# A woven mixer in a two-block transformer kernel: the order of the input blocks, the order within each engine's queue, and where the recurrent steps stand

## What is computed

```python
h = rmsnorm(x, mix_pre_gain)
proj = einsum('bsd,de->bse', h, w_in)                 # 2048 -> 5376
q_a, k_a, v_a, q_r, f_r, i_r, g_r = split(proj)       # 1024,128,128, then 4 x 1024
attn = rmsnorm(sliding_window_attention(q_a, k_a, v_a, sinks), attn_out_gain)   # 16 heads of 64
# recurrent part, 8 heads of 128
f = lb + (1 - lb) * sigmoid(f_r); log_f = log(f); key = 1 - f; qf = silu(q_r); vf = i_r
# per head: outputs o from decayed products of qf and key with vf and a carried state
o = o * rsqrt(mean(o * o) + EPS) * norm_gain
rnn = o * silu(g_r)
mixed = einsum('bse,ed->bsd', concatenate([attn, rnn]), w_out)
x = x + rmsnorm(mixed, mix_post_gain)
```

## Time and profile before

| | |
|---|---|
| time, median of 3 runs (range) | 2494.46 us (2490.78 to 2499.16) |
| the profiled execution's own time, and its span | 2494.21 us, 2492.4 us |
| granted TensorE clock, mean | 0.977 of 2.4 GHz |
| busy: PE, DVE, ACT, POOL | 96%, 59%, 46%, 2% |
| chain that ended last, by engine | PE 85%, issue 7%, DVE 4%, ACT 2%, DMA 1% |

### The profile page before, as it was taken

How to read it: one execution, slowest core, us unless ns; L and a number is a source line. 1 busy time by engine, 2 the same in 40 slices (tenths; PEclk the granted TensorE clock), 3 DMA queues, 4 the chain that set the end, 5 groups by cost and what they waited for, 6 DMA issues and landing times.

```text
span 2492.4 us, 33962 instructions
## 1 busy us (share of the span) xinstructions
PE 2389.5 (96%) x12206; PEld 1997.0 (80%) x12206; DVE 1461.0 (59%) x1849; ACT 1151.8 (46%) x1612; POOL 42.7 (2%) x65
## 2 busy tenths in 40 slices
PE   6999977999999999999999998989999999999997
PEld 5888856888888888888888786778888888888886
DVE  4444367557777546777566566765666544566544
ACT  4444245445555435555454454444544434444442
POOL 1000100000000000000010000000000000000000
PEclk9999878999999999999999899999999999999999
DMA  7666341646556665665655342336566666666652
GB/s 231 192 193 186 92 152 36 194 144 186 177 184 194 194 192 178 187 193 191 202 157 182 93 145 76 102 111 203 153 191 183 192 192 190 187 183 189 208 192 101
DMA packets 311149, 419.19 MB, mean 168 GB/s; under 512 B 15518, under 2 KB 206312, under 8 KB 310292
## 3 DMA queue, kind: packets, MB, share of 16 engines
q1 hardware_dynamic: 308032, 407.09, 53.5%
q0 software_dynamic: 2448, 8.75, 1.1%
q10 hardware_dynamic: 580, 2.20, 0.2%
HBM read 415.86 MB, written 2.12 MB: 168 GB/s over the span
## 4 chain that ended last, share of the span: by engine, by line
PE 85%; issue 7%; DVE 4%; ACT 2%; DMA 1%; POOL 0%; DVEq 0%; SPq 0%; POOLq 0%; ACTq 0%
PE PS L1521 22%; PE PS L1487 12%; PE PS L1486 12%; PE PS L1485 12%; PE PS L1522 11%; PE PS L1717 4%; PE PS L1718 2%; PE PS L1730 1%; PE PS L1732 1%; PE PS L1731 1%; PE PS L1811 1%; DVE x L1076 1%; ACT work L760 1%; PE PS L1539 1%; DMA stage<-in_w_in 1%
## 5 line engine op out<-in xcount | busy, mean ns | idle before, releaser
L1521 PE MATMUL PS<-actT,whi 128*128 128x512 f32 x2432 | 861.3, 398 | 2.8 <-DVE wlo L961 2.8
L932 DVE TENSOR_TENSOR wlo<-stage,whi 128x1024 fp32r<-128x1024 f32 (+1 forms) x367 | 440.1, 1204 | 485.1 <-ACT whi L596 485.1
L1522 PE MATMUL PS<-actT,wlo 128*128 128x256 f32 x2432 | 683.9, 281 | 0.0
L596 ACT ACTIVATE whi<-stage 128x1024 fp32r<-128x1024 f32 (+1 forms) x367 | 381.3, 1042 | 544.0 <-PE PS L1487 519.2
L1521 PEld LDWEIGHTS PS<-actT,whi 128*128 128x128 f32 x2432 | 457.9, 188 | 116.5 <-DVE wlo L961 3.4
L961 DVE TENSOR_TENSOR wlo<-stage,whi 128x1024 fp32r<-128x1024 f32 x298 | 362.7, 1223 | 239.2 <-ACT whi L654 239.0
L654 ACT ACTIVATE whi<-stage 128x1024 fp32r<-128x1024 f32 x298 | 315.9, 1061 | 322.2 <-PE PS L1522 308.4
L1522 PEld LDWEIGHTS PS<-actT,wlo 128*128 128x128 f32 x2432 | 457.3, 188 | 0.1
L1487 PE MATMUL PS<-whi,gT 128*128 128x512 f32 x864 | 340.4, 394 | 0.0
L1486 PE MATMUL PS<-wlo,gT 128*128 128x512 f32 x864 | 338.7, 392 | 0.0
L1485 PE MATMUL PS<-whi,gT 128*128 128x512 f32 x864 | 335.2, 388 | 0.0
(11 more groups left out here) (288 smaller groups left out, 2239.9 us busy)
## 6 DMA issues: line engine op xcount, KB each, us to landing
stage<-in_w_up SPq DMA_DIRECT2D x304, 512.0 KB, 3.8
stage<-in_w_down SPq DMA_DIRECT2D x216, 512.0 KB, 4.1
stage<-in_w_in SPq DMA_DIRECT2D x168, 512.0 KB, 3.7
stage<-in_w_out SPq DMA_DIRECT2D x64, 512.0 KB, 4.4
stage<-in_cmp_k_w SPq DMA_DIRECT2D x8, 512.0 KB, 4.2
stage<-in_cmp_v_w SPq DMA_DIRECT2D x8, 512.0 KB, 5.4
x<-in_x ACTq DMA_DIRECT2D x2, 1024.0 KB, 7.0
grow<-bias_by_distance POOLq DMA_DIRECT2D x2, 1024.0 KB, 7.8
```

Of the source, the lines that this page charges most:

```text
L596: nc.scalar.activation(whi[:, s % SPLITS, 0:wd], stage[:, s % STAGES, 0:wd], ACT.Copy)\
L932: nc.vector.tensor_tensor(wlo[:, s % SPLITS, 0:wd], stage[:, s % STAGES, 0:wd], whi[:, s % SPLITS, 0:wd].bitcast(F32), ALU.subtract).then_ ...
L1521: nc.tensor.matmul(o, whi[:, j % SPLITS, at], actT[:, k, :], start=k == 0, stop=False)
L1522: last = nc.tensor.matmul(o[:, S:2 * S], wlo[:, j % SPLITS, at], actT[:, k, 0:S], start=False, stop=k == KC - 1)
```

## The change

- The order of the blocks: all eight forget and query blocks follow the attention's queries (tiles 24 to 55), then both halves of IR (56 to 71), then the gates (72 to 87). The banks of the last three blocks and the waits for them follow.
- `WINDOW_AT`: a head every 3/2 tiles from 24 (last at 46), before every 5/4 from 25 (last at 43). `STEP_AT`: step r at 63 + 7r/5 (63 to 84), before 57 to 82 with a gap in the middle. Its last `values` and `o_out` come after the loop.
- The two sets of sigmoids stand at 53 and 60 (before 52 and 68), logs at 55 and 62, PE's transposes of them at 55 and 61.
- In ACT's and DVE's loops the mixer operations come ahead of the copies of an ended block.
- `turn_mix2` for p = 0 and 1 moves from the last tile to positions 84 and 86, both into bank 0, and ACT and DVE split these four chunks in iterations 87 and 89. The sigmoid of the first gates moves from 86 to 88, that of the second behind the loop.

```diff
-IN2_BLOCKS = [("tok", C_KA, 256)] + [("feat", C_QA + 256 * i, 256) for i in range(4)] + [("tok", C_IR, NW)]
+IN2_BLOCKS = [("tok", C_KA, 256)] + [("feat", C_QA + 256 * i, 256) for i in range(4)]
 for _i in range(4):
     IN2_BLOCKS += [("feat", C_FR + 256 * _i, 256), ("feat", C_QR + 256 * _i, 256)]
-IN2_BLOCKS += [("tok", C_IR + NW, NW), ("tok", C_GR, NW), ("tok", C_GR + NW, NW)]
+IN2_BLOCKS += [("tok", C_IR, NW), ("tok", C_IR + NW, NW), ("tok", C_GR, NW), ("tok", C_GR + NW, NW)]
...
-IN2_BANKS = [(2 * (k % 2), 2 * (k % 2) + 1) for k in range(14)] + [(0, 3), (2, 0), (3, 2)]
-WINDOW_AT = {25 + 5 * s // 4: s for s in range(HA)}
-STEP_AT = {n: r for r, n in enumerate((57, 59, 60, 62, 63, 65, 66, 68, 72, 73, 75, 76, 78, 79, 81, 82))}
-MIX2_BANK = (4, 5, 6, 7, 2, 3, 4, 5)
+IN2_BANKS = [(2 * (k % 2), 2 * (k % 2) + 1) for k in range(14)] + [(0, 2), (3, 0), (2, 3)]
+WINDOW_AT = {24 + 3 * s // 2: s for s in range(HA)}
+STEP_AT = {63 + 7 * r // 5: r for r in range(16)}
+MIX2_BANK = (0, 0, 6, 7, 2, 3, 4, 5)
...
+                if n - 7 in STEP_AT:
+                    o_out(STEP_AT[n - 7])
+                if n - 3 in STEP_AT:
+                    decays(STEP_AT[n - 3])
+                if n - 5 in WINDOW_AT:
+                    window_turned(WINDOW_AT[n - 5])
+                if n - 4 in WINDOW_AT:
+                    window_exp(WINDOW_AT[n - 4])
+                if n == 52:
+                    attention_squares()
+                if n in (53, 60):
+                    sigmoids(n // 60)
+                if n in (55, 62):
+                    logs(n // 62)
+                if n in (58, 64):
+                    logs_turned(n // 64)
+                if n in (87, 89):
+                    split_turned("mix2", range(n - 87, n - 85), MIX2_BANK)
+                if n == 88:
+                    gate_sigmoid(0)
                 ended = in2_end(n - 3)
                 if ended in FEAT_NO:
                     low_sums2(ended)
                 if ended in TOK_NO:
                     tokens_out(ended)
...
+            o_out(HR * TT - 1)
+            gate_sigmoid(1)
...
-            split_turned("mix2", range(12), MIX2_BANK)
+            split_turned("mix2", range(4, 12), MIX2_BANK)
...
-                if n in (54, 70):
-                    logs_turn(n // 70)
+                if n in (55, 61):
+                    logs_turn(n // 61)
...
-                if n == IN2_TILES - 1:
-                    for p in range(2):
-                        turn_mix2(p)
+                if n in (84, 86):
+                    turn_mix2((n - 84) // 2)
                 in2_tile(n)
+            values(HR * TT - 1)
             for p in range(2, 6):
                 turn_mix2(p)
```

More of the change, by code:

```diff
@@ L802, in tokens_out @@
                 for t in range(TT):
-                    if t == 0 and k >= 14:
-                        act.wait_ge(ev("first_half"), k - 13)
+                    if t == 0 and k >= 13:
+                        act.wait_ge(ev("first_half"), k - 12)
                     else:
@@ L810, in sigmoids @@
             def sigmoids(g):
-                act.wait_ge(ev("in2_feat"), 4 + 4 * (g + 1))
+                act.wait_ge(ev("in2_feat"), 8 + 4 * g)
                 hs = slice(4 * g, 4 * g + 4)
@@ L1404, in _ @@
                     root_of_x(3, 6)
-                ended = in2_end(n - 3)
-                if ended in FEAT_NO:
-                    join2(ended)
                 if n == 12:
@@ L1419, in _ @@
                     front2(WINDOW_AT[n - 3])
-                if n == 51:
+                if n == 53:
                     attention_root()
-                if n == 53:
+                if n == 55:
                     attention_scaled()
[L1424 to L1427, removed]
+                if n in (53, 60):
+                    forgets(n // 60)
+                if n in (56, 63):
+                    keys(n // 63)
                 if n - 5 in STEP_AT:
@@ L1431, in _ @@
                     products(STEP_AT[n - 3])
[L1432 to L1437, removed]
-                    gated(0)
+                if n == 80:
+                    mean_square(0, hstat[:, 0, 0:8], hstat[:, 1, 0:8], P, "o_out", 8)
+                if n in (87, 89):
+                    split_turned("mix2", range(n - 87, n - 85), MIX2_BANK)
+                if n == 88:
+                    gate_silu(0)
+                if n == 89:
+                    gated(0)
+                ended = in2_end(n - 3)
+                if ended in FEAT_NO:
+                    join2(ended)
+            mean_square(0, hstat[:, 0, 8:16], hstat[:, 1, 8:16], P, "o_out", 16)
+            gate_silu(1)
             def last_chunks(j):
@@ L1443, in last_chunks @@
                     split_turned("mix2", range(12, KC), MIX2_BANK)
-            split_turned("mix2", range(8), MIX2_BANK)
+            split_turned("mix2", range(4, 8), MIX2_BANK)
             gated(1)
@@ L1701, in in2_tile @@
                     pe.wait_ge(ev("in2_join"), FEAT_NO[12] + 1)
-                elif j == 0 and k == 16:
-                    pe.wait_ge(ev("in2_tok"), 2 * TOK_NO[14] + 2)
+                elif j == 0 and k > 14:
+                    pe.wait_ge(ev("in2_tok"), 2 * TOK_NO[k - 2] + 2)
                 elif k < 14 and j == 0 and k >= 2:
@@ L1720, in in2_tile @@
                     for t in range(TT):
-                        if t == 1 and j == 0 and k == 14:
-                            pe.wait_ge(ev("in2_join"), FEAT_NO[13] + 1)
-                        if t == 1 and j == 0 and k > 14:
+                        if t == 1 and j == 0 and k >= 14:
                             pe.wait_ge(ev("in2_tok"), 2 * TOK_NO[k - 1] + 1)
@@ L1732, in in2_tile @@
                             last = nc.tensor.matmul(o, al, h, start=False, stop=at_k == KC - 1)
-                        if t == 0 and j == 7 and k >= 14:
+                        if t == 0 and j == 7 and k >= 13:
                             last.then_inc(ev("first_half"), 1)
@@ L1752, in logs_turn @@
                 else:
-                    pe.wait_ge(ev("fac"), 8)
+                    pe.wait_ge(ev("logf_out"), 1)
                 for t in range(TT):
@@ L1790, in exponents @@
                     pe.wait_ge(ev("mix2_in"), 64)
-                if r % 8 == 0:
-                    pe.wait_ge(ev("logf_out"), r // 8 + 1)
-                    pe.wait_ge(ev("key_done"), r // 8 + 1)
+                if r == 0:
+                    pe.wait_ge(ev("logf_out"), 2)
+                    pe.wait_ge(ev("key_done"), 2)
                 if r >= 1:
@@ L1834, in turn_mix2 @@
                 if p == 0:
-                    pe.wait_ge(ev("fac"), HR * TT)
+                    pe.wait_ge(ev("in2_tok"), 8)
+                if p == 1:
+                    pe.wait_ge(ev("actlo_mix2"), 2)
                 if p == 2:
@@ L1839, in turn_mix2 @@
                     pe.wait_ge(ev("in2_tok"), 10)
-                if p >= 6:
-                    pe.wait_ge(ev("actlo_mix2"), 2 * (p - 5))
+                if p == 6:
+                    pe.wait_ge(ev("fac"), HR * TT)
                 pe.wait_ge(ev("mixed2"), 2 if p < 4 else p // 2 + 1)
```

## The result

The changed kernel takes 2459.57 us (median of 4 runs, 2457.81 to 2461.18) against 2494.82 for the kernel before beside it (4 runs); the ratio is 0.9864 with a 95% interval of 0.9844 to 0.9883. The forecast was 2460. The profiled execution has a span of 2459.4 us and took 2461.2.

The account below looks back on a forecast made before the run. PE, busy 96% of the span, was taken as the bound, so gains come from its waits and low clock: 23.1 + 13.0 - 1.5 = 34.6 us off 2494.2 gives 2459.6, say 2460; range 2453 to 2478.

Parts of the forecast that it names:

- Waits, 23.1 less 1.5 for new ones: PE's waits in windows (7.2), steps (12.9) and before the output product (3.0) go; 1.5 us of new short waits come.
- eight lines: The list of PE's waits on other engines in the kernel before, summing to 23.1 us.
- Clock, 13 us (12 to 15): Window and step stretches: PE's low clock follows waits and goes with them, gaining 13 us, bounds 12 to 15.
- The order of the queues: ACT and DVE loops: mixer operations ahead of block copies remove the windows' 7.2 us of waits, bounds 5.7 to 7.2.
- Turns: Before the output product: turning and splitting four chunks earlier removes PE's wait of 3.0 us, bounds 1.5 to 3.0.
- Blocks and sets out of the steps: Step stretch: moving feature blocks and second sigmoid set out removes waits of 8.1, 1.6 and 0.8 us.
- the spacing of the windows: Window stretch: heads every 3/2 tiles instead of 5/4 remove the 1.5 us wait on DVE's wout.
- Cover at position 61: Second logarithm set: ACT needs 8.9 us, PE arrives after 11.0, slack 2.1 us, so nothing waits.
- A: Rival, windows: clock falls whatever the waits, from small matmuls and transposes; gain 25.2 us, time 2469; chance 0.14.
- B: Rival, steps: DVE becomes what PE waits for; 15 us of the gain lost, time 2475; chance 0.12.
- C: Rival: no effect, PE loses the same time to other waits one copy later; 2490 to 2498 us; chance 0.03.
- D: Rival, steps: low clock takes the stretch, costing 59 us over half of positions 63 to 88; 2519 us; chance 0.05.

Follow-up runs that it names:

- e3: Changed kernel with the first four chunks turned ahead of the last tile and split after the loop, as before; stage 340.7 us against 338.4.
- e6: Changed kernel with a recurrent step at every tile from 63 to 78, sixteen in a row; stage 337.6 us against 338.4.
- e10: Same kernel as e7 run again, on one chip with the changed kernel; 2451.43 us against 2456.0, ratio to before 0.9822.
- e12: Same kernel as e2, profiled a second time; 2477.1 us, stage 361.0 us.
- e2: Changed kernel with the old queue order, block copies ahead of mixer operations in both loops; 2475.54 us in one run, stage 357.3 us.
- e1: Kernel before with only the new queue order, mixer operations ahead of block copies; 2468.09 us against 2491.3, ratio 0.9908, stage 348.2 us.
- e4: Changed kernel with the old window spacing, a head every 5/4 tiles from 25; stage 338.36 us.
- e8: Kernel before with one swap in ScalarE's loop, o_out ahead of the next step's decays; 2492.75 us, stage 369.4 us.
- e5: Changed kernel with PE's second transposes of the logarithms at position 59, not 61; stage 343.7 us against 338.4.
- e7: Changed kernel with chunks 12 to 15 turned ahead of the output product's fifth tile, not its seventh; 2449.03 us, ratio to before 0.9834.

## Why the prediction was right

The forecast was a gain of 34.6 us; the medians give 35.3 and the profiled stage 38.2. Term by term:

- **Waits, 23.1 less 1.5 for new ones.** Right: all eight lines are gone. The 0.75 us at tile 3 is not the change's: it stands in nine of the fourteen profiles, the second one of before among them, and is absent from the first of before, e3, e6, e10 and e12. The allowance of 1.5 was not needed.
- **Clock, 13 us (12 to 15).** In the profile that I read the stage had 30.7 us at 0.50, which cost at most 15.4 (the rest, 15.8, less 0.17 for each of twelve waits is 13.8); in a second profile of the same kernel 20.5, at most 10.2. The bounds were for one profile; the term varies by 5 us between runs, more than they allowed. That it goes to zero with the waits was right in every profile without a long wait. That each wait has such a price was wrong as a rule, as e2 shows.
- **The sum came out closer than its terms.** In the profiles, 3.6 us too little in the stage met a late start of the profiled stage of 5.2 us. The start ranged from 1281.2 to 1289.1 us over fourteen profiles with the same code ahead of it, so agreement within 1 us is partly luck, and the forecast of 34.6 should be held to the stage's 38.2 (34.1 between the second profiles).
- **Which part does what.** The order of the queues was the main cause, as argued, and carries more than I had given it: of the waits I had put 7.2 + 2.4 = 9.6 us down to it, and e1 without any other part lost 14.9 (23.1 less the 5.2 among the steps and the 3.0 before the output product). In stage that is 28.4 us added to before, and 18.9 or 22.6 taken out of the changed kernel (e2, e12), so the parts don't simply add. Turns 3.0, as computed (e3). Blocks and sets out of the steps: what is left of 38.2, 9.8 us behind e1, less 3.0 for the turns, so 6.8, made up of e1's 5.2 us of waits among the steps and its rest of 1.6. This one is a difference, not a run of its own, and it doesn't tell the blocks from the sets. I had put 10.5 us of waits down to it (8.1, 1.6 and 0.8).
- **A wrong reason with no effect on the sum.** I put the 1.5 us on `wout` down to the spacing of the windows. The spacing does nothing (e4); in e1 these waits go with the old spacing. The chain of before shows DVE's join of a block (L1275, L1279) directly ahead of `wout`:

```profile
1418.06 0.69 DVE QRT L1279
1418.76 0.40 DVE wout L1333 x2
1419.15 0.14 issue
1419.29 0.52 PE PS L1776 x3
```

- **Cover at position 61.** Computed 2.1 us; in the changed kernel the logarithm ends near 1482.0 and PE's transposes start at 1483.93, 1.9 us. e5 took two tiles (5.5 us) away and showed a wait of 3.5, so 2.0. The Trainium skill's "ScalarE: Activation LUTs", What ACT_TABLE_LOAD costs, gives a drain for each switch of tables, by which e5's wait would have been 6.2 us (an estimate from its 1380 ns); the runs don't show that drain.
- **Rivals.** A (the clock falls in the windows for the small matmuls and transposes themselves): with all of them in place and no waits it stands at 1.00 in the changed kernel, e1, e4 and e6, so what Part 4 of the Trainium skill's "TensorE: Matmul & The Clock Gate" says of transposes explains no fall here. B (DVE): refuted by e6 even at the closest spacing. C (it does nothing) is refuted by the result; its idea, that a removed wait uncovers another, held in e8 and in part in e1. D needed a fall of the clock in the steps without a wait; none occurred.

## What to carry to other kernels

In a hand-woven schedule, put into each engine's queue first what another engine waits for next, and behind it the copies that only free a buffer needed much later; here that was 28 of 38 us of the stage by the first profiles, 23 of 35 by the medians. A wait on a queue may have a second layer: after swapping the operation that showed, look at which engine is late next (e8) before counting the whole wait as gained. When PE's waits go, count their clock as well, but as a spread over several profiles, not as one number.

## What the runs showed of the hardware

The price that a wait has in clock is not set by the wait. The same program with the same waits (23.1 us, and 23.1 with one more of 0.8) had 30.7 and 20.5 us at the low level in its stage, and e2 and e12, again one program, had 3.4 and 13.7; in the output product one wait of 3.5 us was followed by a piece of 103.3, 104.8, 106.0 or 107.8 us, which less the waits and e7's plain 98.1 (99.5 less 1.46 of waits) is 0.2 to 4.7 us; the grant was 1.00 throughout in the two pieces of 103.3, so the 0.2 there is not the clock. In e2 eight waits of up to 1.7 us passed in the window stretch with the grant at 1.00. What decides, from run to run, whether a given wait pulls the clock down was not found.

A wait also costs about 0.17 us beyond PE's idle time without any change of clock (e1: 1.06 us lost, 0.89 idle), since in a stream the next matmul starts 0.23 us after the one before, which counts as busy for 0.40.
